# Norms of the queries, keys and the second branch: sums per token on columns, roots and reciprocals on 3 to 30 columns, spread back by products

## What is computed

```python
def rms_norm(x, g):
    xf = x.astype(jnp.float32)
    return (xf * lax.rsqrt(jnp.mean(xf * xf, -1, keepdims=True) + RMS_EPS) * g).astype(x.dtype)

# mixing_sublayer
qa = rms_norm(aq.reshape(B, T, ATTN_KV_HEADS, ATTN_GROUP, HEAD_DIM), p['qk_norm_g'][0])   # 8 heads of 64
ka = rms_norm(ak.reshape(B, T, ATTN_KV_HEADS, HEAD_DIM), p['qk_norm_g'][1])               # 2 heads of 64
out_a = map_query_blocks(lambda q: _gqa_block(q, keys_a, vals_a), rope(qa))
out_b = map_query_blocks(lambda x1, x2: _diff_block(x1, x2, k1, k2, vals_b, lam), q1, q2)
out_b = rms_norm(out_b, p['diff_subln_g']) * (1.0 - lam_init)                             # 4 heads of 128
```

## Time and profile before

| | |
|---|---|
| median of 3 runs | 2820.94 us (2819.6 to 2821.5) |
| profiled execution: span of the trace | 2814.6 us |
| what the timed runs have beyond the span | 6.3 us |
| PE busy | 2590.3 us (92%) |
| PE weight loads | 2390.9 us (85%) |
| DVE busy | 1433.1 us (51%) |
| ACT busy | 1062.3 us (38%) |
| POOL busy | 329.8 us (12%) |

### The profile page before, as it was taken

How to read it: one execution, slowest core, us unless ns; L and a number is a source line. 1 busy time by engine, 2 the same in 40 slices (tenths; PEclk the granted TensorE clock), 3 DMA queues, 4 the chain that set the end, 5 groups by cost and what they waited for, 6 DMA issues and landing times. The chain is left out here.

```text
span 2814.6 us, 56249 instructions
## 1 busy us (share of the span) xinstructions
PE 2590.3 (92%) x23158; PEld 2390.9 (85%) x23158; DVE 1433.1 (51%) x2322; ACT 1062.3 (38%) x1713; POOL 329.8 (12%) x316
## 2 busy tenths in 40 slices
PE   5999999899789988999979999989987799899998
PEld 3889999887678878999968898988877688789997
DVE  3334365555677645443343335665466766454434
ACT  3333244343533324432253323434444343243322
POOL 0000121000023214000100001300000333030001
PEclk8999999998889998999989999999988899989999
DMA  8766534232200012446466654332312000234463
GB/s 273 242 217 198 161 100 113 83 92 61 63 14 3 4 54 79 129 129 194 127 211 217 222 184 134 110 97 80 92 53 61 3 3 26 60 94 128 124 209 103
DMA packets 482184, 319.92 MB, mean 114 GB/s; under 512 B 15474, under 2 KB 438920, under 8 KB 481800
## 3 DMA queue, kind: packets, MB, share of 16 engines
q1 hardware_dynamic: 481928, 316.32, 37.0%
HBM read 311.30 MB, written 4.98 MB: 112 GB/s over the span
## 5 line engine op out<-in xcount | busy, mean ns | idle before, releaser
L827 PE MATMUL acc<-xm_hi,w_hi 128*128 128x384 f32 x2512 | 876.1, 349 | 54.3 <-DVE xm_lo L2040 33.4
L829 PE MATMUL acc<-xm_hi,w_lo 128*128 128x384 f32 x2512 | 857.7, 341 | 0.0
L828 PE MATMUL acc<-xm_lo,w_hi 128*128 128x384 f32 x2448 | 835.0, 341 | 0.0
L2030 DVE TENSOR_TENSOR w_lo<-raw,w_hi 128x1024 fp32r<-128x1024 f32 (+1 forms) x420 | 519.7, 1237 | 501.0 <-ACT w_hi L1480 493.5
L827 PEld LDWEIGHTS acc<-xm_hi,w_hi 128*128 128x128 f32 x2512 | 486.2, 194 | 98.3 <-issue 57.9
L1480 ACT ACTIVATE w_hi<-raw 128x1024 fp32r<-128x1024 f32 (+1 forms) x420 | 438.8, 1045 | 307.1 <-PE acc L829 219.8
L829 PEld LDWEIGHTS acc<-xm_hi,w_lo 128*128 128x128 f32 x2512 | 485.4, 193 | 0.0
L828 PEld LDWEIGHTS acc<-xm_lo,w_hi 128*128 128x128 f32 x2448 | 472.4, 193 | 1.5
L827 PE MATMUL acc<-h_hi,w_hi 128*128 128x384 f32 x704 | 242.4, 344 | 9.1 <-DVE w_lo L2030 9.1
L828 PE MATMUL acc<-h_lo,w_hi 128*128 128x384 f32 x704 | 239.6, 340 | 0.0
L829 PE MATMUL acc<-h_hi,w_lo 128*128 128x384 f32 x704 | 239.6, 340 | 0.0
(11 more groups left out here) (337 smaller groups left out, 3374.7 us busy)
## 6 DMA issues: line engine op xcount, KB each, us to landing
raw<-in_ffn_w_in SPq DMA_DIRECT2D x179, 512.0 KB, 3.9
modw<-in_w_mod SPq DMA_DIRECT2D x71, 1024.0 KB, 6.1
raw<-in_w_in SPq DMA_DIRECT2D x114, 512.0 KB, 4.1
raw<-in_ffn_w_out SPq DMA_DIRECT2D x64, 512.0 KB, 4.7
raw<-in_ffn_w_out SPq DMA_DIRECT2D x32, 384.0 KB, 3.5
raw<-in_w_up SPq DMA_DIRECT2D x24, 512.0 KB, 3.5
modx<-in_w_mod SPq DMA_DIRECT2D x9, 1024.0 KB, 12.6
raw<-in_w_out SPq DMA_DIRECT2D x16, 512.0 KB, 4.1
```

What stands on the lines that cost most here:

```text
L827: pe.matmul(out, lhs[0], rhs[0], start=first, stop=False)
L828: pe.matmul(out, lhs[0], rhs[1], start=False, stop=False)
L829: return pe.matmul(out, lhs[1], rhs[0], start=False, stop=last)
L2030: done(dve.tensor_tensor(w_lo[:, c % SPL, 0:w], raw[:, c % RAW, 0:w], w_hi[:, c % SPL, 0:w].bitcast(F32), ALU.subtract), lo_done)
```

## The change

The sum of squares is no longer made by a product that leaves it on every channel. The squares become the weights of the product and a column of ones (or two columns, one for each head, `heads2`) is what is streamed, so that the sum of a token lands on that token's partition: 2 columns for each of 3 groups of 128 tokens and each of 5 tiles, 30 in all, for queries and keys; 3 for a tile of the second branch. ACT takes the root of these columns, DVE their reciprocal, and PE spreads them back over the channels by products with the identity (`expand` with 64-column weights for two heads, `spread` with 128-column weights for one). DVE then scales the tile from that bank.

For queries and keys the squares move to the first projections: a sum follows each of them, one root and one reciprocal serve all five tiles, and the loop with the rotations has five turns in place of six. In the second branch the spread stands between the filler and `weigh`, in bank `pb2`, which is the bank that `turn` writes next.

```diff
+                    def head_sums(i):
+                        pe.wait_ge(qsq_ready, i + 1)
+                        for c in range(NCH):
+                            mm = pe.matmul(pb[1][:, 6 * i + 2 * c:6 * i + 2 * c + 2], t1[:, c * 128:(c + 1) * 128], heads2,
+                                           start=True, stop=True)
+                        mm.then_inc(rms_sums, 1)
...
-                    for i in range(6):
-                        if i < 5:
-                            project(B_QK[i])
-                            pe.wait_ge(qsq_ready, i + 1)
-                            pe.matmul(pb[1][:, 0:TOK], blk, t1[:, :], start=True, stop=True).then_inc(qms_done, 1)
+                    pe.wait_ge(rms_inv, 1)
+                    for i in range(5):
                         if i >= 1:
                             pe.wait_ge(qn_ready, i)
-                            if i >= 3:
-                                pe.wait_ge(rope_ready, i - 2)
-                            rotate(i - 1, pb[2 + (i - 1) % 2]).then_inc(rot_done, 1)
+                        expand(pb[1], rq[:, i, :, :], 0).then_inc(rms_spread, 1)
+                        project(B_QK[i])
+                        pe.wait_ge(qn_ready, i + 1)
+                        if i >= 2:
+                            pe.wait_ge(rope_ready, i - 1)
+                        rotate(i, pb[2 + i % 2]).then_inc(rot_done, 1)
...
                         if u >= 1:
                             pe.wait_ge(probs_t_ready, u)
+                        if u >= 2 and units[u - 2]["last"] and units[u - 2]["tile"] >= NB:
+                            pe.wait_ge(sub_done, units[u - 2]["tile"] - NB + 1)
                         for k in range(1 if un["c"] == 0 else 3):
...
                         pe.wait_ge(sub_sq, un["tile"] - NB + 1)
-                        pe.matmul(pb[3][:, 0:TOK], ones, t1[:, :], start=True, stop=True).then_inc(sub_ms, 1)
+                        token_sums(0, t1, True).then_inc(rms_sums, 1)
+
+                    def sub_spread_out(un):
+
+                        pe.wait_ge(rms_inv, 1 + un["tile"] - NB + 1)
+                        pe.wait_ge(probs_t_ready, min(un["u"] + 2, len(units)))
+                        spread(pb[2], rsub).then_inc(rms_spread, 1)
...
                         for key in fillers[u]:
                             filler(key)
+                        if u >= 2 and units[u - 2]["last"] and units[u - 2]["tile"] >= NB:
+                            sub_spread_out(units[u - 2])
                         if u >= 1:
                             weigh(units[u - 1])
...
+                        if i >= 1:
+                            act.wait_ge(rms_sums, i)
+                        done(act.activation(t1[:, :], qk[:, i, :], ACT.Square), qsq_ready)
                     ahead(("av", 0))
+                    act.wait_ge(rms_sums, 5)
+                    done(act.activation(rq[:, :, :, :].rearrange("p i c h -> p (i c h)"), pb[1][:, 0:30], ACT.Sqrt,
+                                        scale=1.0 / HD, bias=eps[:, 1:2]), rms_std)
...
-                        act.wait_ge(sub_ms, un["tile"] - NB + 1)
-                        done(act.activation(t3[:, :], pb[3][:, 0:TOK], ACT.Sqrt, scale=1.0 / 128, bias=eps[:, 1:2]), sub_std)
+                        act.wait_ge(rms_sums, 5 + un["tile"] - NB + 1)
+                        done(act.activation(rsub[:, :], pb[3][:, 0:NCH], ACT.Sqrt, scale=1.0 / 128, bias=eps[:, 1:2]), rms_std)
...
-                            dve.wait_ge(qstd_done, i + 1)
-                            link(dve.reciprocal(t3[:, :], t2[:, :]))
...
+                        dve.wait_ge(rms_spread, i + 1)
+                        gq = par[:, 172:173] if i < 4 else par[:, 173:174]
+                        done(dve.scalar_tensor_tensor(out=qk[:, i, :], in0=qk[:, i, :], scalar=gq, in1=pb[1][:, 0:TOK],
+                                                 op0=ALU.mult, op1=ALU.mult), qn_ready)
+                        ahead(B_QK[i])
+                        rope(i, pb[2 + i % 2])
...
-                        dve.wait_ge(sub_std, k)
-                        link(dve.reciprocal(t3[:, :], t3[:, :]))
-                        done(dve.scalar_tensor_tensor(out=t2[:, :], in0=t2[:, :], scalar=small[:, 4:5], in1=t3[:, :],
+                        dve.wait_ge(rms_std, 1 + k)
+                        done(dve.reciprocal(rsub[:, :], rsub[:, :]), rms_inv)
+
+                    def sub_scale(un):
+
+                        k = un["tile"] - NB + 1
+                        dve.wait_ge(rms_spread, 5 + k)
+                        done(dve.scalar_tensor_tensor(out=t2[:, :], in0=t2[:, :], scalar=small[:, 4:5], in1=pb[2][:, 0:TOK],
                                                  op0=ALU.mult, op1=ALU.mult), sub_done)
```

More of the change, by code:

```diff
@@ L349, in build @@
                 st = sb("st", [128, 4, 4], ctx=ph)
+                rq = sb("rq", [128, 5, NCH, 2], ctx=ph)
+                rsub = sb("rsub", [128, NCH], ctx=ph)
             with ExitStack() as ph:
@@ L403, in build @@
         pads, cin_ready, csum_ready, cmix_ready = (sem(n) for n in ("pads", "cin_ready", "csum_ready", "cmix_ready"))
-        qk_ready, qsq_ready, qms_done, qstd_done, qn_ready = (
-            sem(n) for n in ("qk_ready", "qsq_ready", "qms_done", "qstd_done", "qn_ready"))
+        qsq_ready, qn_ready = sem("qsq_ready"), sem("qn_ready")
+        rms_sums, rms_std, rms_inv, rms_spread = (sem(n) for n in ("rms_sums", "rms_std", "rms_inv", "rms_spread"))
         rot_done, rope_ready, swap_done, swap_ready = (sem(n) for n in ("rot_done", "rope_ready", "swap_done", "swap_ready"))
@@ L411, in build @@
         tile_read, branch_hi, branch_ready = (sem(n) for n in ("tile_read", "branch_hi", "branch_ready"))
-        sub_sq, sub_ms, sub_std, sub_done = (sem(n) for n in ("sub_sq", "sub_ms", "sub_std", "sub_done"))
+        sub_sq, sub_done = sem("sub_sq"), sem("sub_done")
         sig_done, gated, merged_done, merged_hi = (sem(n) for n in ("sig_done", "gated", "merged_done", "merged_hi"))
@@ L980, in _ @@
                         project(("c", i))
-                    for i in range(4):
+                    def head_sums(i):
[4 more added lines that the diff above has]
+                        mm.then_inc(rms_sums, 1)
+                    project(("aq", 0))
+                    for i in range(1, 4):
                         project(("aq", i))
+                        head_sums(i - 1)
                     project(("ak", 0))
+                    head_sums(3)
                     project(("av", 0))
+                    head_sums(4)
                     pe.wait_ge(lam_in, 32)
@@ L1079, in weigh @@
                         if un["first"] and tile > NB:
-                            pe.wait_ge(sub_std, tile - NB)
+                            pe.wait_ge(rms_std, 1 + tile - NB)
                         elif un["first"] and tile >= 1:
@@ L1150, in _ @@
                     pe.wait_ge(lora_act, 2)
-                    def expand(bank, by, col):
-                        for c in range(NCH):
-                            for hh in range(2):
-                                mm = pe.matmul(bank[HALVES[hh], c * 128:(c + 1) * 128],
-                                               by[:, c, col + hh:col + hh + 1].to_broadcast([128, CH]), ident, start=True, stop=True)
-                        return mm
                     def prepare_norm(j):
@@ L2174, in _ @@
                     take_values(0)
+                    dve.wait_ge(rms_std, 1)
+                    flat = rq[:, :, :, :].rearrange("p i c h -> p (i c h)")
+                    done(dve.reciprocal(flat, flat), rms_inv)
                     dve.wait_ge(lam_b, 1)
@@ L2202, in rope @@
                         done(dve.tensor_tensor(qk[:, i, TP:TOK], rt[:, 0, :], rt[:, 1, :], ALU.add), rope_ready)
-                    for i in range(6):
-                        if i < 5:
-                            ahead(B_QK[i])
-                            dve.wait_ge(qstd_done, i + 1)
-                            link(dve.reciprocal(t3[:, :], t2[:, :]))
-                            gq = par[:, 172:173] if i < 4 else par[:, 173:174]
-                            done(dve.scalar_tensor_tensor(out=qk[:, i, :], in0=qk[:, i, :], scalar=gq, in1=t3[:, :],
-                                                     op0=ALU.mult, op1=ALU.mult), qn_ready)
-                        if i >= 1:
-                            rope(i - 1, pb[2 + (i - 1) % 2])
+                    for i in range(5):
+                        dve.wait_ge(rms_spread, i + 1)
[4 more added lines that the diff above has]
+                        rope(i, pb[2 + i % 2])
                     for key in B_QK[5:]:
@@ L2308, in _ @@
                     sub_norm(units[-1])
+                    sub_scale(units[-1])
                     sub_low(units[-1])
```

24 lines of the change are left out of this document (10 added, 14 removed).

## The result

| | before | after |
|---|---|---|
| median of four runs on one chip | 2820.27 us (2817.22 to 2821.50) | 2794.44 us (2793.00 to 2795.25) |
| span of the profiled execution | 2814.6 us | 2789.3 us |
| PE busy | 2590.3 us | 2592.2 us |
| DVE busy | 1433.1 us | 1390.9 us |

The ratio is 0.9913 (95%: 0.9899 to 0.9927). By the medians the change saves 25.8 us where 16.8 were forecast, by the ratio 24.5. Half a microsecond is less than the changed kernel's own four runs are apart, so the time lies on the range's edge.

What follows compares the result with a forecast made beforehand. PE's stream was taken to bound the kernel. Gains of 3.5 + 1.4 + 0 + 0 + 1.1 + 2.4 = 8.4 us a layer, 16.8 for both, took 2820.9 to 2804 us; range 2795 to 2814.

Steps and rivals of the forecast that it cites:

- What bounds the kernel: Whole kernel: PE, busy 92% of the span, sets the time; gains come from removing its work or its waits.
- Queries and keys, 3.5 us a layer: Queries and keys: 10.8 us of products, waits and slowness removed, 7.25 us of small products added; 3.5 us a layer gained.
- the small allowance of 0.1: Cached keys after the queries' last sum: DVE's reciprocal delays their copy 0.75 us, PE comes 0.65 later; 0.1 us.
- rival C: Handovers and queries' loop: waits move, slow stretches stay, nothing else is won; 2812 to 2815 us, chance 0.14.
- The round trip at the handovers: Second branch's handovers: spread and two new waits cost 2.7 us each; gain 1.4 at the first, about nothing at the others.
- Behind the last tile, 1.1 us: Behind the branch's last tile: shorter root and reciprocal, less a new spread of 1.6 us; gain 1.1 of 6.60 us.
- The clock at the handovers: Slow products behind the handovers' long waits: between 0 and 4.8 us a layer regained, half taken, 2.4.
- B: Handovers: the clock returns in full and waits around the spread are shorter; 2797 to 2794 us, chance 0.20.
- A: The forecast: queries' gain as summed, handovers even, part of the clock back; 2798 to 2811 us, chance 0.60.
- D: Handovers: a longer chain through DVE makes the kernel slower, from 2.8 us more at each of six; chance 0.06.

Runs made afterwards that it cites:

- e2: The kernel before with only the second branch's part of the change, queries and keys as before: 2801.35 us, ratio 0.9943.
- e9: The changed kernel with the small products of sums and spreads for queries and keys issued twice in each layer: 2808.90 us, ratio 0.9970.
- e11: The changed kernel with unused products in the waits behind the last tile and sixteen at the third mixer's start: 2781.25 us, ratio 0.9871.
- e1: The kernel before with only the queries and keys' part of the change, second branch as before: 2805.02 us, ratio 0.9956.

## Why the prediction was off, step by step

**What bounds the kernel:** right. The gain came from waits of PE and the slow products behind them, and from nothing else; PE's busy time even rose.

**Queries and keys, 3.5 us a layer:** right. The stages gave 3.67 and 4.33, and with the queries alone the units' stage stayed as it was. The three products' 0.65 and the six's 0.80 held by row (0.58 and 0.65, and 0.81) and by the doubling. A turn takes 5.60 us, 0.2 more than the 5.4 of the sum's parts, and in one place PE now waits 1.39 us for DVE's copy of the cached keys, close to the 1.3 that the same wait had before, as the small allowance of 0.1 had it. What the clock does behind that wait is chance: in the first profile the first twelve spread instructions in the loop take 0.87 us, in the second 1.53, and the slow stretch costs 1.6 us there. That is the slow stretch in the queries' loop of which rival C speaks; it shows once in the four layers of the two profiles.

**The round trip at the handovers:** right in size, off in split. For the second and third handover 1.3 + 0.6 us of waiting were worked out; 1.13 + 0.65 and 1.39 + 0.65 were found. At the first the spread waited only 0.76, so that its gain without the clock is 1.8 and not 1.4. The waits for the probabilities vanished as said.

**Behind the last tile, 1.1 us:** the term was sized too small. From the last sum to the branch's first product were 8.24 us (760.53 to 768.77) and are 6.50 (753.07 to 759.57): 1.74. Root, reciprocal and spread made their part as worked out: the two short instructions give 0.32 and 2.37, and the slow spread with its hop takes 1.8. The rest, 0.8, is the sum itself. ACT comes to its table load 1.73 us behind the sum's start before and 0.91 after, because the sum is no longer slow; the text had the sum's cost unchanged.

**The term sized wrong: the clock at the handovers.** The text took 4.8 us a layer as the upper bound and half of it, 2.4, as the value, "since no wait is as long as the shortest that it replaces, but twice 1 us lies close together". What the runs showed in its place: in the traced execution two waits of up to 1.4 us in 3 us leave the granted clock at 1.00 in all three stretches between the sums, and the term is 2.2 + 1.5 us at the first two handovers, 3.7 us in the first layer, and 0.8 more in the last sum. The kernel that only fills the waits shows the same size by another way, 3.7 and 3.8 us for the units' stage. So the slow stretches went, nearly as the upper bound had it, but that is in part luck. In five traced executions with the branch's part of the change and its waits as they are (two profiles of the changed kernel and runs e2, e9 and e11, two layers each), the first and the second handover were at full speed all 20 times, and the third took 18.0 us four times and 19.5 to 19.6 us six times: there the slow stretch comes back and takes 1.6 us. The half of the text was too low, and its doubt was not unfounded.

**The second term: nothing was counted downstream of the last tile.** The last stage gained 3.43 and 3.23 us a layer where 1.1 was forecast; 0.6 of the difference is the last tile's. The rest, 1.5 to 1.7, is time in the third mixer that no term had. In the changed kernel the 27 us from 785.50 have a granted clock of 0.68, those from 794.00 before 0.62. It is only in part a firm gain: in the changed kernel profiled again the stage gained 2.65 and 3.29 us, and with the queries alone, where nothing in this stage was edited, it took 0.7 us more in one layer and 1.7 less in the other. Where the slow stretches fall in stages that nobody edited changed their length by up to 3 us, and why is not settled. This is also the part of the 25.8 us that the forecast could not have had from its rows.

**The rivals.** B gave 2794 to 2797 with a chance of 0.20, and its main condition, the clock coming back in full at the handovers, is what happened in the first profile. Its sum is not quite its range: 10.8 a layer and 1 us more make 2797, and no term leads to 2794. Its second condition, shorter waits because ACT and DVE run ahead, held at the first handover only. A was the likeliest by the value chosen for one unknown. C fell: the waits did not move. D fell for this kernel, but its threshold, 2.8 us more at each handover, was of the right size: 2.55 more at eight places made it slower than before.

**The range** ended half a microsecond above the median. Its low end stopped short of rival B's 2794, which had a chance of 0.20, and it had no allowance for the up to 3 us by which stages move that nothing was done to.

## What to carry to other kernels

Price a wait of the matrix engine by what its clock does behind it, from that wait's own rows (the distance between equal products before and after it), and not by its length: here a wait of 4.1 us cost 6.3. When a long wait is split into two short ones with work between, expect most of the slow stretches to go and not all (here 24 of 30 handovers were at full speed), look at more than one traced execution, and price the clock cheaply by putting unused products into the old wait. Sums that leave one number per token saved time on the engines behind PE here and none on PE itself, so they pay only where those engines are waited for; put the short reciprocal first on its engine (9.0 us here), since the handover's gain hangs on that chain.

## What the hardware showed that was not expected

Unused products made kernels faster three times, by 16.5, 25.4 and 14.1 us, always with PE busy for longer: those in the 12.2 us wait of the third mixer account for 9.9 us of the 25.4, between the medians, on two chips, of the two kernels before that differ in nothing else. Two waits of 1.39 and 0.65 us, with 1.15 us of work between, left the clock at 1.00, and in another execution of the same program waits of 1.42 and 0.64 us at the same place did not (0.91 from sum to sum, slow products from 742.6 to 746.2): the same waits and the same work do not always get the same clock. It goes for long waits too: with the queries alone (e1), the second layer's wait of 2.63 us at the second handover has no slow product behind it, and the stretch from sum to sum takes 21.69 us at 1.00 in place of 23.25. Behind the waits of 4.10 and 2.64 us two stretches of the kernel before had less:

```profile
733.84:738.00 4.16, 4.16 (x19) 3.87 (x20) 3.40 (x11) 2.91 (x7) 0.00 (x0) 0.72 0.35 118
...
709.76:713.76 4.00, 4.00 (x15) 3.44 (x16) 3.12 (x10) 2.56 (x7) 0.00 (x0) 0.50 0.28 80
```

The 4 us behind the longer wait (second row) are all at the lower level; behind the shorter one the first products are fast and only those from 735.6 to 739.0 slow, so a slow stretch need not begin where the wait ends. A product with 2 columns costs PE 105 ns an instruction, where one of a projection with 384 costs 174.
